# Sliding attention: the probabilities are scaled by their inverse sums on GpSimd instead of VectorE

## What is computed

```python
def sink_softmax(s, mask, sink):
    s = jnp.where(mask, s.astype(jnp.float32), NEG_INF)
    m = jnp.maximum(jnp.max(s, axis=-1, keepdims=True), sink)
    p = jnp.exp(s - m)
    return p / (jnp.sum(p, axis=-1, keepdims=True) + jnp.exp(sink - m))
...
    p = sink_softmax(s, mask, sink_b[None, :, :, None, None, None])
...
    o_real = jnp.einsum('bkgnqs,bknsd->bkgnqd', p.astype(v.dtype), v_band).reshape(B, N_KV_HEADS, GROUP, S, HEAD_DIM)
...
    return o @ w_out
```

## Time and profile before

| what | value |
|---|---|
| median of 3 runs | 1764.68 us (1760.96 to 1765.32) |
| the profiled execution | 1766.55 us, its span 1764.6 us |
| TensorE busy | 1729.7 us, 98% |
| VectorE busy | 1055.8 us, 60% |
| ScalarE busy | 726.5 us, 41% |
| GpSimd busy | 21.2 us, 1% |
| mean granted clock of TensorE | 0.991 |

### The profile page before, as it was taken

The page is one execution under the profiler, slowest core; times in us unless marked ns, Lnnn a source line. Parts: engine busy times, 40 slices in busy tenths (PEclk is TensorE's granted clock), DMA queues, the critical chain, the costliest instruction groups (busy, mean ns, idle before and its releaser), DMA issues.

```text
span 1764.6 us, 31401 instructions
## 1 busy us (share of the span) xinstructions
PE 1729.7 (98%) x12344; PEld 1401.9 (79%) x12344; DVE 1055.8 (60%) x1915; ACT 726.5 (41%) x1179; POOL 21.2 (1%) x26
## 2 busy tenths in 40 slices
PE   9999999999999999999999999999999999999997
PEld 8999989899999999997899999998953333333332
DVE  7775575787755887568787656867762232222223
ACT  6434463464344544355654436957531101110110
POOL 0000000100000000000000001000020000000000
PEclk9999999999999999999999999999999999999998
DMA  6545334445454355531245645443889999999996
GB/s 245 185 178 192 131 122 151 69 150 190 174 202 149 143 191 209 179 137 73 96 167 192 224 161 193 146 159 120 326 328 426 427 427 428 428 428 428 428 427 260
DMA packets 42342, 409.73 MB, mean 232 GB/s; under 512 B 5304, under 2 KB 5304, under 8 KB 7056
## 3 DMA queue, kind: packets, MB, share of 16 engines
q1 hardware_dynamic: 40032, 402.21, 58.3%
q0 software_dynamic: 1936, 5.79, 1.6%
q10 hardware_dynamic: 288, 0.52, 0.1%
HBM read 405.87 MB, written 2.63 MB: 232 GB/s over the span
## 4 chain that ended last, share of the span: by engine, by line
PE 87%; DMA 6%; DVE 4%; ACT 2%; issue 1%; SPq 0%; DVEq 0%; ACTq 0%
PE ps L613 85%; PE ps L617 2%; DMA branch<-w_gate_up 2%; DMA late<-w_gate_up 2%; DMA soon<-w_gate_up 1%; DVE w_lo L1802 1%; DMA raw<-w_units 1%; ACT w_hi L1327 1%; DVE branch L1844 0%; ACT arena L1574 0%; ACT arena L1591 0%; DVE x_lo L1865 0%; DVE h L1855 0%; DVE branch L1831 0%; DVE arena L2191 0%
## 5 line engine op out<-in xcount | busy, mean ns | idle before, releaser
L613 PE MATMUL ps<-x_hi,w_hi 128*128 128x256 f32 (+1 forms) x2144 | 615.2, 287 | 4.4 <-DVE x_lo L1865 1.8
L613 PE MATMUL ps<-x_lo,w_hi 128*128 128x256 f32 (+1 forms) x2144 | 610.4, 285 | 0.0
L613 PE MATMUL ps<-x_hi,w_lo 128*128 128x256 f32 (+1 forms) x2144 | 608.9, 284 | 0.0
L1802 DVE TENSOR_TENSOR w_lo<-raw,w_hi 128x1024 fp32r<-128x1024 f32 (+1 forms) x352 | 447.9, 1293 | 126.5 <-ACT w_hi L1327 125.7
L1327 ACT ACTIVATE w_hi<-raw 128x1024 fp32r<-128x1024 f32 (+1 forms) x352 | 385.8, 1114 | 196.3 <-PE ps L613 111.2
L613 PEld LDWEIGHTS ps<-x_hi,w_hi 128*128 128x128 f32 x2144 | 403.7, 188 | 11.6 <-issue 5.5
L613 PEld LDWEIGHTS ps<-x_hi,w_lo 128*128 128x128 f32 x2144 | 405.6, 189 | 0.0
L613 PEld LDWEIGHTS ps<-x_lo,w_hi 128*128 128x128 f32 x2144 | 404.6, 189 | 0.3
L613 PE MATMUL ps<-hid_hi,w_hi 128*128 128x272 f32 (+1 forms) x704 | 200.8, 285 | 0.0
L613 PE MATMUL ps<-hid_hi,w_lo 128*128 128x272 f32 (+1 forms) x704 | 200.0, 284 | 0.0
L613 PE MATMUL ps<-hid_lo,w_hi 128*128 128x272 f32 (+1 forms) x704 | 199.4, 283 | 0.0
(11 more groups left out here) (343 smaller groups left out, 2016.2 us busy)
## 6 DMA issues: line engine op xcount, KB each, us to landing
raw<-w_units SPq DMA_DIRECT2D x144, 1024.0 KB, 4.8
soon<-w_gate_up SPq DMA_DIRECT2D x32, 2048.0 KB, 21.7
late<-w_gate_up SPq DMA_DIRECT2D x24, 2048.0 KB, 21.0
raw<-w_out_units SPq DMA_DIRECT2D x32, 1408.0 KB, 6.1
soon<-w_down SPq DMA_DIRECT2D x16, 2048.0 KB, 24.7
late<-w_down SPq DMA_DIRECT2D x12, 2048.0 KB, 22.1
branch<-w_gate_up SPq DMA_DIRECT2D x8, 2048.0 KB, 22.6
branch<-w_down SPq DMA_DIRECT2D x4, 2048.0 KB, 20.4
```

Source lines behind the costliest of these rows:

```text
L613: return nc.tensor.matmul(out_ap, lhsT, rhs, start=start, stop=stop, skip_group_check=True)
L1802: v.tensor_tensor(part(w_lo, c, 0, n), raw_slot(u, j * n, n), part(w_hi, c, 0, n).bitcast(F32), ALU.subtract).then_inc(lo_made, 1)
```

## The change

The four multiplications of a group leave VectorE's queue and stand in GpSimd's, in a loop over the eight groups between the DMAs of L582 and the wait for `stat11`. VectorE's reciprocal increments a new semaphore, `sink_inverse`, for which GpSimd waits once a group. GpSimd increments `p_ready` after each multiplication, as VectorE did; TensorE's waits are the same. The other user of this `attend` (the block attention of the second block, whose scaling is on ScalarE) keeps its semaphore `inverse_made`.

```diff
--- before.py
+++ after.py
@@ -335,6 +335,7 @@
         x_ready, h_ready = sem("x_ready"), sem("h_ready")
         act_chain, dve_chain = sem("act_chain"), sem("dve_chain")
         soft_made, decay_in, decay_made = (sem(n) for n in ("soft_made", "decay_in", "decay_made"))
+        sink_inverse = sem("sink_inverse")
         q_roped, neg_max, exp_made, p_ready = (sem(n) for n in ("q_roped", "neg_max", "exp_made", "p_ready"))
         lb_in, lb_exp = sem("lb_in"), sem("lb_exp")
         hg_arg, hg_ln, lvl_in, lvl_exp, lvl_ready = (
@@ -581,6 +582,15 @@
                 with nc.allow_non_contiguous_dma(reason="gains in the order of the gathered tiles"):
                     pool.dma_start(small[:, 272 + 8 * i:280 + 8 * i].rearrange("p (a k) -> p a k", k=4),
                                    ln1_rows[0, i * D:(i + 1) * D].rearrange("(a f k) -> f a k", a=2, k=4)).then_inc(ln1_cols, 16)
+            for g in range(8):
+                at = 16 + (g % 3) * 16
+                pool.wait_ge(sink_inverse, g + 1)
+                for u in range(4):
+                    n, b = divmod(u, 2)
+                    a, size = b * SWA_ROW + n * (P + META), SWA_ROW - P - META if n else P + META
+                    p = a_p[g % 3][:, a:a + size]
+                    nc.gpsimd.tensor_scalar(p, p, small[:, at + 12 + u:at + 13 + u], None, ALU.mult).then_inc(p_ready, 1)
+
             t = plan["stat11"].at(0)
             pool.wait_ge(full[t[0]], t[1] + 1)
             pool.wait_ge(bias_out, 16)
@@ -2244,15 +2254,8 @@
                     if sinks:
                         then(v.tensor_tensor(small[:, at + 8:at + 12], small[:, at + 8:at + 12],
                                              small[:, at + 4:at + 8], ALU.add))
-                    if not sinks:
-                        v.reciprocal(small[:, at + 12:at + 16], small[:, at + 8:at + 12]).then_inc(inverse_made, 1)
-                        return
-                    then(v.reciprocal(small[:, at + 12:at + 16], small[:, at + 8:at + 12]))
-                    for u in range(4):
-                        n, b = divmod(u, 2)
-                        a = b * row + n * second
-                        p = pbs[g % 3][:, a:a + (row - second if n else second)]
-                        v.tensor_scalar(p, p, small[:, at + 12 + u:at + 13 + u], None, ALU.mult).then_inc(p_ready, 1)
+                    v.reciprocal(small[:, at + 12:at + 16], small[:, at + 8:at + 12])\
+                        .then_inc(sink_inverse if sinks else inverse_made, 1)
 
                 for g in range(2):
                     maxima(g)
```

## The result

| kernel | median | runs | ratio to before, 95% interval |
|---|---|---|---|
| before | 1763.83 us | 1760.96 to 1765.32 | |
| changed | 1772.86 us | 1771.32 to 1779.46 | 1.0058, 1.0045 to 1.0071 |

The changed kernel is slower by 9.0 us between medians, about half a per cent. By the ratio it is 10.2 us, with an interval of 7.9 to 12.5. The forecast was 1769.4, in a range of 1764.8 to 1777.0.

The account below looks back on a forecast made before the run. TensorE was taken to bound the middle of the edited attention, waiting for scalings at both ends. Delays of 0.98 us (group 0) and 3.77 (group 7) made about +4.7 on 1764.68: 1769.4 us, range 1764.8 to 1777.0.

Parts of the forecast that it names:

- The bound and the gain: Edited attention: TensorE paces the middle groups, so removing 32 scalings (1.04 us a group) from VectorE gains 0.
- signs of being wrong: Scalings over 0.7 us each on average, free overlap with the weight split, or a second stretch at half clock.
- The price of a scaling: GpSimd's four scalings a group, 832 columns at 2.30 ns: 1.92 us, between bounds of 1.04 and 4.04.
- The handover: From VectorE's inverse to GpSimd's first scaling: 0.14 us, 0.10 more than VectorE following its own inverse.
- The groups: Delay by group: +0.98 in 0, nothing in 1 and 2, +0.38 in 3, +1.08 in 4, 5 covered, +3.77 at 7.
- on the side: Group 6: transposes 2.44 us later, but not on the path, as exponents(7) wait for outputs(4), which come before them.
- The lock: VectorE instructions with two SBUF inputs and GpSimd's exclude each other: 1.22 us before group 4's scalings, 1.3 in group 7.
- C: Rival: a start cost per GpSimd instruction, four scalings taking 2.12 to 4.04 us; over 5.3 us, up to +13.2; chance 0.25.
- E: Rival: waits in groups 4, 6 and 7 let TensorE's clock fall again, 3.3 us more, 1772.7 us; chance 0.15.
- B: Rival: GpSimd scales as fast as VectorE, unhindered, +0.2 us; dearer variant with the lock +2.1; chance 0.15 together.
- F: Rival: faster, if TensorE's end waits were for VectorE's queue and earlier maxima help; at most 1 us; chance 0.03.
- The likeliest case: Whole kernel: "same", a change within about 0.3% (5.3 us) that a measurement can't tell from none; chance 0.52.

Follow-up runs that it names:

- e2: Kernel before with only groups 1 to 5 scaled on GpSimd, groups 0, 6 and 7 on VectorE: 1768.13 us, +4.4 over the kernel before.
- e10: Kernel before with only groups 1, 2 and 5 on GpSimd, each as two TENSOR_TENSOR over paired blocks: 1765.45 us, +2.3 over the kernel before.
- e6: Changed kernel with VectorE's weight split moved from behind group 4's inverse to behind group 1's: 1771.22 us, +8.4 over the kernel before.
- e7: Changed kernel with idle matmuls on TensorE before the transposes and in the last query rotations: 1772.9 us, +10.1 over the kernel before.
- e4: Changed kernel with two TENSOR_TENSOR a group over paired blocks in place of four TENSOR_SCALAR: 1767.38 us, +3.6 over the kernel before.

## Why the prediction was right or wrong

The bound and the gain: right. TensorE paces the stage, and taking 32 scalings off VectorE brought nothing forward.

The range holds the result, and the forecast's 4.7 is half of what was measured. Two of the signs of being wrong that I had set came: the scalings take over 0.7 us each (3.14 for four), and the clock's row shows a second stretch at half.

The price of a scaling: this is the step that failed. I took 1.92 us for four by the two-operand row and argued that one operand less and four starts would cancel. They take 3.14: 0.63 for 144 columns and 0.95 for 272 where nothing holds them, which is 2.5 ns a column and 0.27 to start. Halves (0.51 for 72 columns, 0.63 for 136) bear out that there is a price to start. And the form is dearer: 272 columns at 0.95 are 3.5 ns a column with the start in it, while the pairs' 544 with two operands took 1.08 in group 0, 2.0 ns a column, and L602's 1024 take 2.3. So one operand less made nothing cheaper, and the starts came on top. The statement of the Trainium skill (GPSIMD Engine Reference, section 4.1) that one-input operations run at roughly line rate doesn't hold for this instruction: four take 3.14 us where VectorE takes 1.04. I rightly kept it out of the sum, but the sum was still too low.

The handover: 0.10 from VectorE's inverse to GpSimd (817.68 to 817.78), forecast 0.14.

The groups, by the differences in the table's first trace: group 0 forecast +0.98, found +2.0. Groups 1 and 2 forecast 0, found 0 and +0.5; e2 and e10 show that group 1 is covered only while TensorE is late or slow. Group 3 +0.38, found +1.1. Group 4 +1.08 with the lock, found +1.3 (in the second trace 3 and 4 together 3.2). Group 5 forecast 0, found +0.2 and +0.6. Group 6 was "on the side" in the forecast, because exponents(7) don't wait for it. They don't, but TensorE's own queue does: its wait there delays outputs(5) and with them transposes(7). Whether group 6 or GpSimd's work on group 7 ends last is decided by little: GpSimd is done with group 7 at 851.50, TensorE with outputs(5) at about 852.0; in e6, at the higher clock, it is the other way round. My own sum with the measured price would be 4.7 + 3 x (3.14 - 1.92) = 8.4 us, close to the medians' 9.0 and 9.8. That is luck in part: with the lock's measured sizes too (below) the same sum is 8.4 - 0.3 - 1.1 = 7.0, which fits the 7.1 and 7.2 of e7 and e6; the rest goes with the clock.

The lock: right in group 4, in the order of events that the earlier trace rows left open. GpSimd lost 0.88 us (4.02 - 3.14), where I had put the split's full 1.2 before its start. Wrong in size in group 7: I added 1.3 us for four blocked scalings and found 0.24 (3.38 - 3.14). There VectorE is the one that is held: its subtractions take 0.54 and 0.59 for 0.42. And one row was misread: L2619 in the earlier trace rows has one input in SBUF and a constant, so it shows nothing of instructions with two inputs, as which I took it. The kernel before does have such a row, right behind it, first without and then beside GpSimd's operations:

```profile
1303.97 1.70 DVE L2615 TENSOR_TENSOR moe<-moe,sg 128x128 f32<-128x128 f32 x8
...
1313.22 2.65 DVE L2615 TENSOR_TENSOR moe<-moe,sg 128x128 f32<-128x128 f32 x2
```

Two take longer there than eight without. The Trainium skill (SBUF — State Buffer, "Who interferes with whom") has an exclusive lock for the whole instruction; group 4 agrees, but against a queue of short instructions the loss was shared, and smaller than that rule times four.

The rivals: C held its ground. Its condition, more than 2.12 us for four, was met, and the result lies between its ends. E, the second fall of the clock, came in both traces of the changed kernel (17 us at half, and twice 3.4); e6 and e7 show 7 us of the loss without it, so it adds 1 to 3 us and isn't the main cause. B and F are out. The likeliest case was within 0.3% and the result is slower by 0.5%; the 0.45 for slower was where it went.

## What to carry to other kernels

Before moving an elementwise step to a slower engine, ask who waits for its last instruction. If that is the engine that paces the kernel, the step's own time is what counts, and emptying the queue it came from is worth nothing unless somebody waits for what stood behind it. Price the step by a row of the same form and about the same size; if there is none, small instructions should be given a start cost of their own, and the outcome multiplied by the places where it is exposed.

## What the runs showed of the hardware

- GpSimd multiplied by a per-partition column in 0.63 (144 columns) and 0.95 us (272) in float32, 2.5 ns a column plus 0.27 us an instruction, but by a broadcast second tensor in 0.66 (288 columns) and 1.08 us (544), as in group 0 of e4: two such instructions did in 1.72 us what four of the other form did in 3.14.
- An instruction of VectorE with two SBUF inputs that came first held GpSimd's next one (4.02 instead of 3.14 us), and the 0.84 to 0.88 us moved with it when it was moved.
- Idle matmuls kept TensorE at its higher clock through the whole stage in one kernel (PEclk 1.00) and failed in another (0.50 from 816 to 820 us), and in neither was the median lower.
